# The down product of each expert ahead of the next expert's whole gate and up product

## The reference

```
D_MODEL, SEQ, DEPTH = 1024, 256, 2
N_EXPERTS, TOP_K, D_EXPERT = 32, 2, 512
...
def expert_block(args):
    xb, e = args
    return (jax.nn.silu(xb @ w_gate[e]) * (xb @ w_up[e])) @ w_down[e]

ys = lax.map(expert_block, (xs, block_e)).reshape(n_slots, d)
ys = ys * slot_gate[:, None].astype(ys.dtype)
return jax.ops.segment_sum(ys, slot_tok, num_segments=n + 1)[:n]
```

## Time and profile before

| | |
|---|---|
| time, median of 3 runs | 1332.42 us (1329.86 to 1334.49) |
| profiled execution, its own time | 1335.83 us |
| its span, first to last instruction | 1333.9 us |
| PE busy | 1222.3 us, 92% |
| DVE, ACT, POOL busy | 446.2, 178.1, 69.0 us |
| mean granted TensorE clock | 0.979 |
| HBM read | 485.04 MB, 364 GB/s over the span |
| first and second half of all experts (line 805) | 2048 matmuls, 480.6 us busy |
| down of all experts (line 824) | 1024 matmuls, 230.8 us busy |
| combine (line 833) | 256 matmuls, 118.4 us busy |

### The profile page before, as it was taken

How to read it: one execution, slowest core, us unless ns; L and a number is a source line. 1 busy time by engine, 2 the same in 40 slices (tenths; PEclk the granted TensorE clock), 3 DMA queues, 4 the chain that set the end, 5 groups by cost and what they waited for, 6 DMA issues and landing times.

```text
span 1333.9 us, 13658 instructions
## 1 busy us (share of the span) xinstructions
PE 1222.3 (92%) x5018; PEld 504.0 (38%) x5018; DVE 446.2 (33%) x905; ACT 178.1 (13%) x375; POOL 69.0 (5%) x84
## 2 busy tenths in 40 slices
PE   6999997889999999899898899999999998998897
PEld 3444443545333333233233267453333333332232
DVE  4296774566212221122112134551222222121112
ACT  2212124622000000000000011220000000000000
POOL 0113100000000000000000000000000000000000
PEclk9999998999999999999999899999999999998999
DMA  9948758465999999999999994759999999999995
GB/s 353 384 184 349 265 210 315 174 272 232 382 422 422 422 423 422 422 422 422 423 422 422 418 406 181 316 218 405 421 422 422 421 423 422 422 422 422 421 422 242
DMA packets 81216, 486.54 MB, mean 365 GB/s; under 512 B 6176, under 2 KB 7712, under 8 KB 32032
## 3 DMA queue, kind: packets, MB, share of 16 engines
q1 hardware_dynamic: 79168, 481.91, 88.5%
q10 hardware_dynamic: 2016, 4.21, 0.9%
HBM read 485.04 MB, written 1.05 MB: 364 GB/s over the span
## 4 chain that ended last, share of the span: by engine, by line
PE 59%; SPq 20%; DMA 13%; DVE 4%; ACT 2%; issue 2%; POOL 0%; DVEq 0%; ACTq 0%; POOLq 0%
PE PS L805 19%; SPq L307 16%; DMA ring<-in_moe_w_up 10%; PE PS L824 10%; PE PS L615 8%; PE PS L833 5%; SPq L312 4%; PE PS L585 2%; PE PS L937 2%; PE PS L957 2%; PE PS L687 2%; DMA ring<-in_ada_w 2%; PE PS L797 2%; PE PS L815 1%; DVE KQH L1702 1%
## 5 line engine op out<-in xcount | busy, mean ns | idle before, releaser
L805 PE MATMUL PS<-ring,KQH 128*64 128x512 f32 x2048 | 480.6, 614 | 33.5 <-DMA ring<-in_moe_w_up 31.9
L805 PEld LDWEIGHTS PS<-ring,KQH 128*64 128x64 f32 x2048 | 146.5, 141 | 314.7 <-issue 277.1
L824 PE MATMUL PS<-ring,KQH 128*64 128x512 f32 x1024 | 230.8, 593 | 0.9 <-ACT KQH L1152 0.9
L824 PEld LDWEIGHTS PS<-ring,KQH 128*64 128x64 f32 x1024 | 73.1, 137 | 146.3 <-issue 144.9
L1685 DVE TENSOR_TENSOR TMP<-PS,TMP 64x512 f32<-64x512 f32 x64 | 44.1, 688 | 232.2 <-PE PS L824 231.2
L1685 DVE TENSOR_TENSOR TMP<-PS,KQH 64x512 f32<-64x512 f32 x64 | 44.1, 688 | 228.9 <-PE PS L824 227.9
L833 PE MATMUL PS<-TMP,KQH 128*128 128x512 f32 x256 | 118.4, 606 | 1.6 <-DVE TMP L1685 1.6
L615 PE MATMUL PS<-ring,KQH 128*128 128x512 f32 x256 | 114.0, 593 | 0.0
L1158 ACT ACTIVATE KQH<-PS 128x256 f32<-128x256 f32 x62 | 23.8, 383 | 669.4 <-PE PS L805 669.4
L1702 DVE TENSOR_TENSOR KQH<-KQH,PS 128x256 f32<-128x256 f32 x64 | 38.7, 605 | 158.3 <-ACT KQH L1158 158.3
L447 POOL COPY KQH<-KQH 128x512 f32 x62 | 38.0, 614 | 839.3 <-PE PS L805 769.7
(11 more groups left out here) (236 smaller groups left out, 779.0 us busy)
## 6 DMA issues: line engine op xcount, KB each, us to landing
ring<-in_moe_w_gate SPq DMA_DIRECT2D x128, 1024.0 KB, 26.2
ring<-in_moe_w_up SPq DMA_DIRECT2D x128, 1024.0 KB, 26.6
ring<-in_moe_w_down SPq DMA_DIRECT2D x64, 2048.0 KB, 28.1
ring<-in_ada_w SPq DMA_DIRECT2D x23, 2048.0 KB, 16.7
ring<-in_attn_w_in SPq DMA_DIRECT2D x2, 4096.0 KB, 12.8
ring<-in_attn_w_in SPq DMA_DIRECT2D x2, 2048.0 KB, 20.9
ring<-in_attn_w_out SPq DMA_DIRECT2D x1, 4096.0 KB, 16.4
ring<-in_pool_w_in SPq DMA_DIRECT2D x1, 4096.0 KB, 25.0
```

The lines of the kernel that those rows point to most:

```text
L805: ins = mm(PS[64 * f:64 * f + 64, 4, :], xs[:, k, 0:SLOTS], gu_w[s][:, :, k, 256 * f:256 * f + 256], start=k == 0, stop=k == KC - 1)
L824: ins = mm(PS[64 * f:64 * f + 64, 6, :], lhs, dn_w[s][:, c, 512 * f:512 * f + 512], start=c == 0, stop=c == 3)
```

## The change

In each step of the loop and in step 31 the waits and the product `down` move ahead of the first half of n; the two halves of n then stand together. Nothing else is edited: no instruction is added or removed on any engine, and the counts that SP waits for stay.

```
                     transposes(None if c % 2 else sg).then_inc(L.tr_done, 1)
-                    if not last:
-                        pe.wait_ge(L.gu_in[L.slot(n)], (2 * it + n // 3) * 32 + 32)
-                        pe.wait_ge(L.xw_ready, e + 1)
-                        gate_up(L.slot(n), xw[n % 2], range(4)).then_inc(L.gu_half, 1)
                     pe.wait_ge(L.t_ready, e + 1)
                     pe.wait_ge(L.dn_in[L.slot(c)], (2 * it + c // 3) * 16 + 16)
                     if c % 2:
                         pe.wait_ge(L.y_v, 2 * e)
                     down(L.slot(c)).then_inc(L.dn_done, 1)
                     if not last:
+                        pe.wait_ge(L.gu_in[L.slot(n)], (2 * it + n // 3) * 32 + 32)
+                        pe.wait_ge(L.xw_ready, e + 1)
+                        gate_up(L.slot(n), xw[n % 2], range(4)).then_inc(L.gu_half, 1)
                         pe.wait_ge(L.gu2_in[L.slot(n)], (2 * it + n // 3) * 32 + 32)
                         gate_up(L.slot(n), xw[n % 2], range(4, KC)).then_inc(L.gu_done, 1)
```

More of the change, by code:

```diff
@@ L888, in step @@
                     transposes(None if c % 2 else sg).then_inc(L.tr_done, 1)
[L889 to L892, removed]
                     pe.wait_ge(L.t_ready, e + 1)
```

## The result

The changed kernel takes 1347.95 us (median of 5 runs, 1340.82 to 1348.60) against 1332.42 us for the kernel before (median of 5 runs too, 1329.86 to 1334.49). The ratio is 1.0098, 95% interval 1.0068 to 1.0127: 1% slower, where 0.4% faster was forecast. The time lies outside the stated range. The profiled execution took 1348.60 us, with a span of 1346.8 us, 12.9 us over that of before.

The account below looks back on a forecast made before the run. The loads, with TensorE's work left after them, were taken to set each layer's end. Tail gain 1.9 less 0.36 plus gap 1.1 gave 2.6 us a layer: 1332.42 - 5.2 = 1327.2 us, range 1323 to 1332.5.

Parts of the forecast that it names:

- the part on the clock: TensorE's 1.97 us stop before down: under about 3 us, so no low stretches (products slowed at 1.2 GHz).
- Rival 3: Clock falls, TensorE becomes the bound: 1.7 us per low stretch, 1339.8 us with 5 in each layer; chance 0.12.
- The copy no longer covered: TensorE waits for ACT's copy before down: odd steps 0.53 us longer, even 0.75, a pair 1.28 us.
- Slack on TensorE: TensorE's 27.81 us per pair of steps stays under the loads' 29.82, so its longer stops cost nothing.
- The gap in the loads: Expert 4's down load goes out 3 us earlier, closing a stall: landings 1.1 us earlier per layer, bounds 0 to 2.0.
- The tail behind the last weights: At expert 31 the second half starts at its weights' landing, silu 3.7 us later: 1.9 us gained per layer, less 0.36.
- The sum without the low stretches: Whole kernel with no low stretches: 2.6 us gained in each layer, 1332.42 - 5.2 = 1327.2 us.

Follow-up runs that it names:

- experiment 1: Changed kernel plus three short products of zeros between transposes and down in every step: 1327.31 us, ratio 0.9955.
- experiment 11: Changed kernel plus three short products of zeros between transposes and down in odd steps only: 1328.41 us, ratio 0.9953.
- experiment 13: Changed kernel plus one short product of zeros between transposes and down in odd steps: 1326.86 us, ratio 0.9948.
- experiment 6: Kernel before, order unchanged, plus five short products of zeros in odd steps' stop for silu: 1333.00 us, ratio 1.0003.
- experiment 4: Kernel before with down first only in steps 1, 29 and 30 of each layer: 1329.81 us, ratio 0.9964.
- experiment 7: Kernel before with down first only in steps 1, 29 and 30, plus five short products in odd steps' stop for silu: 1331.20 us, ratio 0.9978.
- experiment 8: Changed kernel plus two short products ahead of down, and ACT's copy in even steps split in two parts: 1324.65 us, ratio 0.9935.
- experiment 2: Changed kernel plus five short products of zeros ahead of the transposes in odd steps, none at the copy: 1328.17 us, ratio 0.9958.
- experiment 14: Changed kernel plus one short product of zeros ahead of the transposes in odd steps: 1327.14 us, ratio 0.9949.

## Why the prediction was wrong

**The step that failed** is the part on the clock. It put the low stretches of the new order at none, because TensorE's new stop of 1.97 us lay between one of 1.5 us, which was never followed by the low level, and one of 3.0 us, which sometimes was the earlier trace rows, and because two stops of 1.97 us behind silu of 31 were spared. Measured were 6 in each layer. Stops of 1.97 us were indeed spared in every trace. But the new ones were 2.05 to 2.26 us, since the copy's stop, taken from step 31 as 0.46 us, is 0.54 to 0.75 us in the loop. (The copy itself takes 0.37 us in both. From its end to down's start it is 0.06 us in step 31 and 0.14 to 0.24 in steps 5 and 3; why is open.) On the sum that error weighs 2 us a layer; by the clock the layer lost 10.6, and the error is what carries two thirds of the odd stops over the edge. The old trace had one stop between, 2.58 us in step 15 of layer 0, and it was spared. With half of them spared later, one case could not tell, so the term had a bound on either side and not a value of none. Rival 3 was this case. Its chance of 0.12 was too small and its arithmetic was right: by it 6 stretches in layer 0 give 757.6 + 6 x 1.7 = 767.8 us, and the undersized stops add 0.14 us a pair, 2.1 us; measured was 770.2.

The Trainium skill, "TensorE: Matmul & The Clock Gate", section "Why this matters for your kernels", tells to avoid gaps over about 3 us, which the prediction took to mean that shorter ones leave the clock alone. These traces don't agree with that: the changed kernel has 12 low stretches behind stops of 2.15 to 2.26 us, none of them with a wait for a load. Nor did the rows agree as the prediction said, unless the transposes count as part of the gap: ahead of the slow product at 588.35 us the idle pieces are 1.12 and 1.52 us. The section "A second HAM failure mode: psum-queue depth-cycling", which tells of frequent short stops in a kernel of another kind, is the one that pointed the right way. What the two transposes inside the stop count for, no run here separates. Why about half of the stops over the edge are spared, and always much the same ones, is open too.

**The copy no longer covered**: forecast 1.28 us a pair, measured 1.43 to 1.46 (27.96 to 27.99 us a pair against 26.53). Right in kind, a little small.

**Slack on TensorE, the second step that failed**: it was forecast that a period of 27.8 under the loads' 29.8 costs nothing, so that loads and tail set the end. But TensorE starts a layer behind the loads: by TensorE alone silu of 31 was forecast at 757.6, by the loads at 760.3. The 2.7 us between them were all the cover that 15 pairs left. The longer stops used 2.2 of them and the earlier landing the rest. In experiments 1, 11 and 13, with no low stretch at all, silu of 31 is 5.1 to 5.3 us behind the last landing and not 4.1, and in experiment 1 no wait for weights is seen where the prediction looked for some at second halves from about expert 26.

**The gap in the loads**: right. The down load of expert 4 went out at 346.1 us, forecast 346.0, and the last weights landed 2.2 us earlier in layer 0, over the upper bound of 2.0, and 1.5 in layer 1, where 1.1 was taken. Not all of the 2.2 need be the gap: in the old order, as it is and filled, they land 415.9 us behind silu of 1 three times (the kernel before in layer 1, experiment 6 in both) and 416.9 once. Against 415.9 the changed kernel gains 1.2 to 1.5 us, close to the forecast. Experiments 4 and 7 show that it takes more than step 1 to close the gap.

**The tail behind the last weights**: hidden in the changed kernel and in experiment 1, in which TensorE was late; in experiment 8 it is there, 3.9 us instead of 3.7.

**The sum without the low stretches** was 1327.2 us; experiments 1, 2, 11, 13 and 14, in which only they are gone, are at 1327.3, 1328.2, 1328.4, 1326.9 and 1327.1. What turned the sign was thus the one side effect on the clock. That the sum comes out so well is partly luck. The kernel before was at 1333.3 to 1334.8 us in those experiments, so the gain was 4.9 to 7.9 us and not 5.2; and in layer 0 of experiment 1 the weights land 1.1 us earlier than forecast and TensorE is 1.1 us later behind them.

## What to carry to other kernels

A reordering that uncovers a wait lengthens a stop, and where that stop joins another one on TensorE the clock may fall for the next products: cost it at what a slow product costs (here 1.7 us) times a share of the steps, unless the trace shows many stops of that length without harm. Here one to three short products in the stop kept the clock up; test this first when a kernel with little slack gets slower by more than its waits. And a period under that of the loads is no slack by itself: ask what is left of it at the last step.

## What the runs showed of the hardware that was not expected

- A stop of TensorE of 2.15 to 2.26 us, with two transposes in it, was followed by the 1.2 GHz level in 46 of 100 cases, one of 1.97 to 2.06 us in 0 of 60, and the kernel before's of 1.44 us in 0 of 14. Two traces of one kernel had the same 12 steps hit.
- One product of zeros of 0.2 us in the stop, at either end, took all 12 low stretches away, worth 16 to 21 us between medians of different chips, though TensorE's other work and its end of the stop were unchanged.
- The kernel that falls to the low level spreads wider from run to run: 1340.2 to 1348.6 us for the changed kernel over its 9 runs, with a mean clock of 0.976 to 0.985, against 1326.7 to 1328.4 us and 0.991 to 0.996 with the stop filled (experiment 1).
